# A two-block transformer stack on one core: the filler matmuls beside its norms are left out

## The reference: what is computed

```python
def rmsnorm(x, g):
    xf = x.astype(jnp.float32)
    y = xf * lax.rsqrt(jnp.mean(xf * xf, axis=-1, keepdims=True) + EPS)
    return (y * g.astype(jnp.float32)).astype(x.dtype)
...
        h = rmsnorm(x, norm_mix_pre[l])
        proj = jnp.einsum('bsd,de->bse', h, w_in[l])
...
        mix = jnp.einsum('bsd,de->bse', merged, w_out[l])
        x = x + rmsnorm(mix, norm_mix_post[l])
        h = rmsnorm(x, norm_ffn_pre[l])
        f = conv_gated_mlp(h, w_up[l], conv_w[l], conv_b[l], w_down[l])
        x = x + rmsnorm(f, norm_ffn_post[l])
```

## Time and profile before

| | |
|---|---|
| median of 3 runs | 3771.73 us |
| lowest and highest run | 3766.18 and 3783.63 us |
| span of the profiled execution, first to last instruction | 3777.3 us |
| TensorE (PE) matmul busy | 3615.8 us, 96% of the span |
| VectorE (DVE), ScalarE (ACT), GpSimd (POOL) busy | 50%, 35%, 8% |
| TensorE's mean granted clock | 0.975 |

### The profile page before, as it was taken

How to read it: one execution, slowest core, us unless ns; L and a number is a source line. 1 busy time by engine, 2 the same in 40 slices (tenths; PEclk the granted TensorE clock), 3 DMA queues, 4 the chain that set the end, 5 groups by cost and what they waited for, 6 DMA issues and landing times.

```text
span 3777.3 us, 41376 instructions
## 1 busy us (share of the span) xinstructions
PE 3615.8 (96%) x16320; PEld 2761.9 (73%) x16320; DVE 1897.7 (50%) x2464; ACT 1331.2 (35%) x1650; POOL 293.5 (8%) x229
## 2 busy tenths in 40 slices
PE   7989999999999899999999998999989999999999
PEld 6565786888765657868887655788868888868887
DVE  4545445554255553455542894555264334455543
ACT  2424223554224242235542323444222122235442
POOL 3111002000121110020001002000010000020000
PEclk9999999999998989999999999999999999999999
DMA  5210232232231102222222111232221222212322
GB/s 141 43 54 12 67 100 78 78 100 84 95 87 31 56 9 74 93 78 81 97 84 95 56 45 34 78 100 89 90 73 57 90 66 67 79 45 89 100 84 73
DMA packets 238180, 278.70 MB, mean 74 GB/s; under 512 B 5310, under 2 KB 205158, under 8 KB 238054
## 3 DMA queue, kind: packets, MB, share of 16 engines
q1 hardware_dynamic: 233410, 264.60, 21.6%
q0 software_dynamic: 3936, 12.06, 1.7%
q10 hardware_dynamic: 708, 0.27, 0.0%
HBM read 274.81 MB, written 2.10 MB: 73 GB/s over the span
## 4 chain that ended last, share of the span: by engine, by line
PE 89%; DVE 6%; POOL 3%; ACT 1%; issue 1%; DMA 0%; POOLq 0%; DVEq 0%; ACTq 0%
PE ps L1202 23%; PE ps L1203 23%; PE ps L1204 23%; PE ps L1360 4%; POOL t_sq L431 3%; PE ps L1339 2%; PE ps L1461 2%; PE ps L1241 2%; PE ps L1243 2%; PE ps L1242 2%; PE ps L1397 2%; PE ps L1510 1%; PE ps L1258 1%; PE ps L1577 1%; PE ps L1264 1%
## 5 line engine op out<-in xcount | busy, mean ns | idle before, releaser
L781 DVE TENSOR_TENSOR t_wlo<-t_wraw,t_whi 128x2048 fp32r<-128x2048 f32 x252 | 586.5, 2327 | 1411.4 <-ACT t_whi L519 1411.4
L519 ACT ACTIVATE t_whi<-t_wraw 128x2048 fp32r<-128x2048 f32 x252 | 482.4, 1915 | 1403.1 <-PE ps L1204 1296.7
L1202 PE MATMUL ps<-t_hh,t_whi 128*128 128x512 f32 x2384 | 947.4, 397 | 10.7 <-DVE t_hl L827 7.3
L1204 PE MATMUL ps<-t_hh,t_wlo 128*128 128x512 f32 x2384 | 941.7, 395 | 0.0
L1203 PE MATMUL ps<-t_hl,t_whi 128*128 128x512 f32 x2384 | 941.5, 395 | 0.0
L1202 PEld LDWEIGHTS ps<-t_hh,t_whi 128*128 128x128 f32 x2384 | 449.2, 188 | 129.1 <-issue 14.5
L1203 PEld LDWEIGHTS ps<-t_hl,t_whi 128*128 128x128 f32 x2384 | 449.0, 188 | 107.0 <-issue 2.0
L1204 PEld LDWEIGHTS ps<-t_hh,t_wlo 128*128 128x128 f32 x2384 | 448.8, 188 | 106.3
L431 POOL TENSOR_TENSOR t_sq<-t_sq 128x512 f32<-128x512 f32 x102 | 170.4, 1671 | 3027.5 <-ACT t_sq L641 1477.3
L1204 PE MATMUL ps<-t_midh,t_wlo 128*128 128x512 f32 x704 | 277.8, 395 | 0.0
L1203 PE MATMUL ps<-t_midl,t_whi 128*128 128x512 f32 x704 | 277.8, 395 | 0.0
(11 more groups left out here) (205 smaller groups left out, 4673.3 us busy)
## 6 DMA issues: line engine op xcount, KB each, us to landing
t_wraw<-in_w_in_dram SPq DMA_DIRECT2D x46, 1024.0 KB, 5.3
t_wraw<-in_w_up_dram SPq DMA_DIRECT2D x44, 1024.0 KB, 5.1
t_wraw<-in_ffn_w_in_dram SPq DMA_DIRECT2D x44, 1024.0 KB, 5.1
t_wraw<-in_w_kv_dram SPq DMA_DIRECT2D x24, 1024.0 KB, 5.2
t_wraw<-in_w_down_dram SPq DMA_DIRECT2D x20, 1024.0 KB, 5.0
t_wraw<-in_ffn_w_out_dram SPq DMA_DIRECT2D x20, 1024.0 KB, 5.0
t_wraw<-in_w_branch_dram SPq DMA_DIRECT2D x12, 1024.0 KB, 5.0
t_wraw<-in_w_q_dram SPq DMA_DIRECT2D x12, 1024.0 KB, 5.2
```

Of the source, the lines that this page charges most:

```text
L519: sc.activation(whi[slot][:, :], wraw[slot][:, :], ACT.Copy).then_inc(w_hi, 1)
L781: v.tensor_tensor(wlo[slot][:, :], wraw[slot][:, :], whi[slot][:, :].bitcast(F32), ALU.subtract).then_inc(w_lo, 1)
L1202: te.matmul(out, wh, xh, start=first, stop=False)
L1204: return te.matmul(out, wl, xh, start=False, stop=last)
```

## The change

All calls of `keep_warm` and the function itself are taken out, and with them the loops in `pre` and in front of the layer norm's `norm`, whose waits on `squared` only paced the fillers. `norm` keeps its own waits. Nothing is added, and nothing changes on another engine.

```diff
-            def keep_warm(n=1):
-
-                for _ in range(n):
-                    te.matmul(bank(5), meanm, base[:, 0:T], start=True, stop=True)
-
             def norm(name, wait=None):
...
                 ins.then_inc(summed, 1)
-                keep_warm(1)
 
                 pe.wait_ge(diagonal, n + 1)
                 te.matmul(bank(b0), meanm, std, start=True, stop=True).then_inc(spread, 1)
-                keep_warm(2)
 
             def out_product(f, bufs, split):
...
-                keep_warm()
                 norm(f"post{2 * f}")
 
             def pre(h):
-                for t in range(KT):
-                    if h and t < KT - 1:
-                        pe.wait_ge(squared, SQUARES[f"pre{h}"] + t + 1)
-                        keep_warm()
                 norm(f"pre{h}")
...
-                keep_warm()
                 norm(f"post{2 * f + 1}")
...
             ln_mean(3)
-            for t in range(KT):
-                pe.wait_ge(squared, SQUARES["ln_var"] + t + 1)
-                keep_warm()
             norm("ln_var")
```

## The result

| | kernel before | kernel with the change |
|---|---|---|
| median of 4 runs each | 3768.95 us | 3803.93 us |
| lowest to highest | 3765.59 to 3783.63 us | 3793.54 to 3808.37 us |
| ratio, with its 95% interval | | 1.0088 [1.0061, 1.0115] |
| span of the profiled execution | 3777.3 us | 3791.7 us |
| time of the profiled execution | not given | 3793.54 us |

The change makes the kernel slower by more than the 0.5% that can be told. The median lies 0.9 us above the upper end of the range, 17 us above the predicted 3787. Two repeats later gave ratios of 1.0059 [1.0036, 1.0082] and 1.0065 [1.0049, 1.0081], with medians of 3796.26 and 3792.76 us, inside the range. Over 16 runs of the changed kernel and 52 of the one before, the means are 3796.8 and 3771.5 us: +25 us, or 0.67%. The single executions of either kernel scatter over some 20 us.

The account below looks back on a forecast made before the run. TensorE, busy 96% of the span, was taken as the bound, except in norms, where a four-engine chain is. The terms summed to +14.8, say +15 us, on 3771.7, giving 3787 us; range 3775 to 3803.

Parts of the forecast that it names:

- first products behind pre1, 3, 4, 5, 7: The first 48 products after these five pre norms (the heads) start at the low clock, 2.3 us each: +11.5 us.
- behind pre6: First products after pre6 come slower, and 1.3 us of slack takes part of the low start's loss: +0.9 us.
- behind pre0, pre2 and ln_var: First products there lose 0: waits on VectorE or GpSimd cover pre0 and pre2, ln_var's start is low already.
- sums of pre norms and ln_var: Four sums now at full clock, 1.95 us, become low ones of 3.11 us, 1.16 us each: +4.6 us.
- post norms behind feed-forward, to the root: Sums in post3, post5 and post7 lose half of 1.16 us each; post1 is low already: +1.8 us.
- spreads: Post7's spreading matmul goes from 1.12 to 1.86 us, +0.7 us; the others are low already or come out even.
- ahead of the out-projections' post norms: In post0, 2, 4 and 6 sums start earlier without a filler in front, about 0.75 us off each: -3.0 us.
- spreads' late start: A low filler ahead of the spread delays it by about 0.24 us, at seven places: -1.7 us.
- Rival 1: First products run at full clock all the same; only what stood in front changes, -4.7 us, about 3767; chance 0.14.
- Rival 2: Low starts are long and nothing covers them: nine heads lose 3.0 us each, +31, about 3803; chance 0.13.
- Rival 3: Low time costs half its length everywhere, in gaps and heads: +64 us, about 3836; chance 0.03.

Follow-up runs that it names:

- r1_head: Changed kernel with 27 of the 116 fillers back, between sums and diagonal and behind the spread, in pre norms and ln_var; ratio 1.0031 to the kernel before.
- r2_after_tbl: Changed kernel with ScalarE's table load moved ahead of the last square in an out-projection's post norm; one run of 3790.65 us.
- r2_dense: Kernel before with 186 fillers, laid closer where TensorE waits and none ahead of ready work; median 3757.79 us, ratio 0.9968 to the kernel before.
- r1_before: Unchanged kernel before, run once more for a second trace; ratio 0.9997 to the kernel before.

## Why the prediction was right and wrong

The mechanism was right: the clock falls in the gaps and products start low; what was gained in front is smaller. The size was too small, +15 us against +25 over all runs and +21 in the norm stages. Two terms were far too low, and part of that was offset by luck, since other terms came out below what I had put. The terms by their measured means of three traces each, in us:

| term of the sum | predicted | measured |
|---|---|---|
| first products behind pre1, 3, 4, 5, 7 | +11.5 | +9.8 (55.5 to 65.3) |
| behind pre6 | +0.9 | +1.0 (12.37 to 13.33) |
| behind pre0, pre2 and ln_var | 0 | -0.4, -0.8 and -0.5 |
| sums of pre norms and ln_var | +4.6 | **+9.3** (22.9 to 32.2) |
| post norms behind feed-forward, to the root | +1.8 | +2.0 |
| spreads | +0.7 | **+3.7** (29.9 to 33.7) |
| ahead of the out-projections' post norms | -3.0 | **-1.5** (10.3 to 8.8) |
| spreads' late start | -1.7 | -1.4 |
| together | +14.8 | +21.2 |

- **The sums of the pre norms were twice as dear.** The step that failed is "3.11 at the low". That row was itself partly at the full clock, as the stretches of the same sums in the trace of before show (0.54 us full, then low). Without fillers all nine sums take 3.57 to 3.58 us, so a full one that becomes low costs 1.6 us and not 1.16. And I counted only the four that stood at 1.95 us. The others, at 2.9 to 3.2 us, were mixtures too and grew to 3.57 as well, all but pre0's, which had 3.58 us already in the trace of before and would have told the true price. Stretches of pre4's sums, and the row of pre0's, both before:

```profile
core 0: us, PE busy (x), PEclk, DMA share, GB/s
2088.68:2089.22 0.54, 0.54 (x5) 1.00 0.00 0
2089.22:2091.80 2.58, 2.58 (x14) 0.50 0.00 0
```

```profile
27.02 3.58 PE L1258 MATMUL ps<-t_base,t_sq 128*128 128x1 f32 x16 [9.59 <-POOL t_sq L431]
```

- **The spreads were taken as even.** The step is "the other spreads are low already or come out even". In the pre norms and ln_var a low spread behind a filler took 1.91 us, and without one it takes 2.07 (`r1_head` shows 1.91 again, at the same low clock): +0.8 us in all. A spread behind a low filler also starts 0.28 us behind the diagonal, and one without it 0.06 us behind. So without the filler the spread ends only 0.06 us sooner, and the two rows of the table have to be read together. In the post norms more of them fall to the low clock than I had counted: 12.0 us together before, 15.0 after, +2.9 us where I had 0.7.
- **The sums' earlier start was capped.** "This takes about 0.75 us off each" left out that ScalarE's table load becomes what is late next. It gave 0.52 us in post0 and post2, 0.42 in post4, and 0.04 in post6. `r2_after_tbl` shows the cap (1.42 to 1.14 us).
- **The heads were priced well,** 2.3 us against 2.0. Every one of the five took 12.4 to 13.8 us, within what I had said to look for (12.7 to 14.0) but for its lower end. `r1_head`, where the heads are back at 55.6 us with the clock full, shows that this term is the clock at the heads. Over the five heads of all thirteen traces (65) the 48 products take 11.05 us and another 0.45 us for each us at the low clock (a fitted line, correlation 0.996).
- **Rival 1 is out:** no head of the changed kernel ran at the full clock; each of the fifteen was low for 2.9 to 6.1 us. **Rival 2 is out** as a mechanism, though its 3803 was nearest to the first median: the stalls of pre0 and pre2 did hide the low start, as predicted (from the last square to the 48th product pre2 takes 23.8 us against 23.2, pre0 30.0 against 30.7, with a scatter of 2 to 3 us). **Rival 3 is out:** the low time in the norm stages rose by 199 us (from 83 to 282) and the time by 21 us, a tenth and not a half. The Trainium skill, page "TensorE: Matmul & The Clock Gate", section "HAM oscillation — how this bites in real kernels", would make it an estimated 99 us, half of 199. The measurement decides: only of the low time that TensorE works through is about half lost, 0.45 in the heads.
- **The chance of slower was too low** (0.35), since the +15 was held against a bound of 19 us while two of its terms, the sums of the pre norms and of the feed-forward's post norms, were priced from a row that was a mixture of both clocks.

## What to carry to other kernels

A filler on TensorE is worth what the useful work just behind it gains in clock, and it costs what it stands in front of. So lay fillers where TensorE waits for another engine, close enough to hold the clock, and take them away ahead of work that is ready. When pricing a clock change, take the low price of each instruction from a row that lies in a low stretch for its whole length, and sum over every instruction, also the short ones that wait on each other: here sums of one column (16 records, 1.95 to 3.57 us) were as dear as the big products.

## What was not expected of the hardware

- Matmuls of one column, each with a weight load of its own, are not too small for the clock to matter, and the records of their weight loads are longer at the low clock too: in the views by source line the median weight load of the sums is 192 ns in the kernel r2_dense, where nearly all are at the full clock, and 333 ns in the changed one, the median matmul 250 and 352 ns. Which of the two sets the pace is not shown. R2_dense first:

```profile
L1258 PEld LDWEIGHTS ps<-t_base,t_sq x272: 186/192/338, 24.7 to 3740.7; 128*128 128x128 f32 x136
L1258 PE MATMUL ps<-t_base,t_sq x272: 164/250/374, 24.7 to 3740.7; 128*128 128x1 f32 x136
```

```profile
L1253 PEld LDWEIGHTS ps<-t_base,t_sq x272: 186/333/338, 24.8 to 3771.8; 128*128 128x128 f32 x136
L1253 PE MATMUL ps<-t_base,t_sq x272: 164/352/374, 24.8 to 3771.9; 128*128 128x1 f32 x136
```

- Executions of one and the same kernel differ by up to 24 us (3759.61 to 3783.70 in twelve runs of r1_before), and the traces put most of it down to how long the attention stages run at the low clock. A single pair of profiles would have given +14 us, the first medians +35; only stages and repeats gave 19 to 25.
